# The routing stage of a mixture-of-experts step: VectorE's and TensorE's order around the last tiles, and where the Sigmoid table is loaded

## The reference

```python
mix = concatenate([rms_norm(attn, w_a), rms_norm(ssm, w_s)])
x = x + mix @ w_out                                  # called x1 here
h = rms_norm(x, norm_ffn_w)
score = sigmoid(h @ w_router)                        # 64 experts
idx = top_k(score + router_bias, 8)
g = 2.5 * score[idx] / sum(score[idx])
x = x + sum_e g_e * (silu(h @ w_gate[e]) * (h @ w_up[e])) @ w_down[e] + shared_expert(h)
```

## Time and profile before

| | |
|---|---|
| median of 3 runs | 1548.09 us (1543.95 to 1552.09) |
| profiled execution | 1553.29 us, span of the trace 1551.5 us |
| busy | PE 1376.6 us (89%), PEld 728.9 (47%), DVE 613.1 (40%), ACT 347.4 (22%), POOL 246.5 (16%) |
| chain that ended last | DMA 25% of the span, PE 20%; of it w_down transfers 24% |
| HBM | read 395.25 MB, written 41.06 MB, 281 GB/s over the span |

### The profile page before, as it was taken

How to read it: one execution, slowest core, us unless ns; L and a number is a source line. 1 busy time by engine, 2 the same in 40 slices (tenths; PEclk the granted TensorE clock), 3 DMA queues, 4 the chain that set the end, 5 groups by cost and what they waited for, 6 DMA issues and landing times. The chain is left out here.

```text
span 1551.5 us, 30198 instructions
## 1 busy us (share of the span) xinstructions
PE 1376.6 (89%) x9894; PEld 728.9 (47%) x9895; DVE 613.1 (40%) x1813; ACT 347.4 (22%) x939; POOL 246.5 (16%) x291
## 2 busy tenths in 40 slices
PE   6999799999999998699879787779999999999982
PEld 3445566666767775344633222223444443333320
DVE  1424255776486663333733222222333333332223
ACT  1202144444434444300101111111111111111110
POOL 1000200005363310000000111111222222211120
PEclk9999899999999999899879988889999999999996
DMA  8312399999989999650086999999875899999966
GB/s 305 66 27 57 104 310 302 349 338 325 318 294 315 336 333 338 231 197 28 7 344 223 371 370 372 372 369 370 326 220 177 297 319 313 380 370 357 370 233 201
DMA packets 160665, 424.08 MB, mean 273 GB/s; under 512 B 48209, under 2 KB 51826, under 8 KB 134386
## 3 DMA queue, kind: packets, MB, share of 16 engines
q1 hardware_dynamic: 142912, 381.30, 67.6%
q0 software_dynamic: 14400, 38.82, 10.4%
q10 hardware_dynamic: 3250, 2.65, 0.5%
HBM read 395.25 MB, written 41.06 MB: 281 GB/s over the span
## 5 line engine op out<-in xcount | busy, mean ns | idle before, releaser
L2555 PE MATMUL ps_gu<-ring,mixT 128*32 128x512 f32 (+2 forms) x1664 | 366.9, 636 | 57.1 <-SPq L2313 56.3
L2555 PEld LDWEIGHTS ps_gu<-ring,mixT 128*32 128x32 f32 (+2 forms) x1664 | 125.8, 141 | 293.6 <-issue 252.8
L2574 PE MATMUL ps_y<-w_dn,aT_e 128*32 128x512 f32 (+2 forms) x832 | 175.9, 598 | 4.5 <-DVE aT_e L2469 2.0
L1496 PE MATMUL ps_kT<-ident,ring 128*128 128x128 f32 x1024 | 142.3, 282 | 9.2 <-DVE ring L1129 4.9
L1496 PEld LDWEIGHTS ps_kT<-ident,ring 128*128 128x128 f32 x1024 | 115.3, 145 | 67.7 <-ACT ring L960 33.9
L2339 POOL DMA_INDIRECT kT<-h_dram,idx x50 | 51.9, 1038 | 583.0 <-DVE idx L2428 583.0
L2467 DVE TENSOR_TENSOR act_in<-sil,ps_gu 128x256 f32<-128x256 f32 x48 | 20.2, 421 | 295.0 <-ACT sil L2387 295.0
L1129 DVE COPY ring<-ps_kT 128x512 f32<-128x512 f32 x128 | 88.2, 689 | 88.1 <-PE ps_kT L1496 85.5
L2387 ACT ACTIVATE sil<-ps_gu 128x256 f32<-128x256 f32 x48 | 18.4, 384 | 401.0 <-PE ps_gu L2555 401.0
L2343 POOL DMA_INDIRECT sums_dram<-qT,sidx x48 | 76.5, 1593 | 147.8 <-DVE qT L2477 143.9
L2574 PEld LDWEIGHTS ps_y<-w_dn,aT_e 128*32 128x32 f32 (+2 forms) x832 | 55.4, 132 | 93.4 <-issue 85.7
(11 more groups left out here) (519 smaller groups left out, 1663.7 us busy)
## 6 DMA issues: line engine op xcount, KB each, us to landing
ring<-in_cache_k SPq DMA_DIRECT2D x256, 256.0 KB, 4.3
ring<-in_cache_v SPq DMA_DIRECT2D x256, 256.0 KB, 4.8
ring<-in_w_gate_e SPq DMA_DIRECT2D x64, 1024.0 KB, 8.8
ring<-in_w_up_e SPq DMA_DIRECT2D x64, 1024.0 KB, 11.8
w_dn<-in_w_down_e SPq DMA_DIRECT2D x64, 1024.0 KB, 9.8
w_in<-in_w_in SPq DMA_DIRECT2D x8, 1028.0 KB, 18.9
sums_dram<-w_dn SPq DMA_DIRECT2D x1, 4608.0 KB, 20.5
ring<-in_w_out SPq DMA_DIRECT2D x1, 4096.0 KB, 15.5
```

Of the source, the lines that this page charges most:

```text
L1496: last = pe.transpose(ps_kT[:, j % 2, e * PAGE:(e + 1) * PAGE], k_places[n % RING][:, e * DA + j * P:e * DA + (j + 1) * P], m.ident[:, :])
L2555: last = pe.matmul(ps_gu[at, :].rearrange("p (g n) -> p g n", g=2), xgT[:, u, k, at], w_gu[:, place, :, k, :].rearrange("p s g n -> p (s g ...
L2574: last = pe.matmul(ps_y[at, n, :], aT[:, j, at], w_dn[:, place, j, n * 512:(n + 1) * 512].rearrange("p s n -> p (s n)"), start=(j == 0), s ...
```

## The change

VectorE now handles x1 of tile t first and the hT copy of tile t-1 right behind it, ahead of the norm of tile t; the copy of the last tile stands after the loop. TensorE does router(3) before the last transposes instead of after. ScalarE gets one activation of one column with Sigmoid ahead of its wait for the router products; its result is written over a value that is no longer read.

```diff
--- before.py
+++ after.py
@@ -1918,6 +1918,7 @@
                         act.wait_ge(h_done, t)
                         if t >= 1:
                             act.wait_ge(h_out[(t + 1) % 2], 16 * ((t + 1) // 2))
+                act.activation(inv[:, 1, 0:1], m.ones[:, 0:1], ACT.Sigmoid)
                 act.wait_ge(iota_done, 1)
                 act.wait_ge(r_mm, TT)
                 act.activation(score[:, 0:PT, :].rearrange("p t e -> p (t e)"), ps[:, 7, 0:PT * NE], ACT.Sigmoid)
@@ -1948,6 +1949,16 @@
                 dve.reciprocal(inv[0:T_S, 2, 2 * PT:], inv[0:T_S, 1, 2 * PT:])
                 dve.wait_ge(misc_in, 32)
                 dve.wait_ge(x_again, 16 * TT)
+
+                def to_hT(t):
+
+                    n = rows(t)
+                    for half in range(2):
+                        dve.wait_ge(tr_mm, 2 * t + half + 1)
+                        c = m.col["norm_ffn"] + 4 * half
+                        w = m.columns[:, c:c + 4].unsqueeze(2).to_broadcast((P, 4, n))
+                        tt(hT[:, 4 * half:4 * half + 4, cols(t)], ps[:, half, :].rearrange("p (k n) -> p k n", n=P)[:, :, 0:n], w, ALU.mult).then_inc(hT_done, 1)
+
                 for t in range(TT):
                     n = rows(t)
                     for half in range(2):
@@ -1958,6 +1969,8 @@
                             at = slice(half * T_S, (half + 1) * T_S) if t == PT else slice(0, P)
                             last = dve.scalar_tensor_tensor(x1, ps[at, 2 + 2 * half + i, :], inv[0:n, 2, 2 * t + i:2 * t + i + 1], x1, ALU.mult, ALU.add)
                         last.then_inc(x1_done, 1)
+                    if t >= 1:
+                        to_hT(t - 1)
                     dve.wait_ge(ss_done, t + 1)
                     dve.tensor_scalar(st[0:n, 1, t:t + 1], st[0:n, 0, t:t + 1], 1.0 / D, EPS, ALU.mult, ALU.add).then_inc(ms2, 1)
                     dve.wait_ge(root2, t + 1)
@@ -1968,11 +1981,7 @@
                     dve.tensor_scalar(xn[0:n, t % 2, :], m.xres[0:n, t, :], st[0:n, 0, t:t + 1], None, ALU.mult).then_inc(xn2, 1)
                     dve.drain()
                     tt(h_row[0:n, t % 2, :], xn[0:n, t % 2, :], ffn_row[0:n, :], ALU.mult).then_inc(h_done, 1)
-                    for half in range(2):
-                        dve.wait_ge(tr_mm, 2 * t + half + 1)
-                        c = m.col["norm_ffn"] + 4 * half
-                        w = m.columns[:, c:c + 4].unsqueeze(2).to_broadcast((P, 4, n))
-                        tt(hT[:, 4 * half:4 * half + 4, cols(t)], ps[:, half, :].rearrange("p (k n) -> p k n", n=P)[:, :, 0:n], w, ALU.mult).then_inc(hT_done, 1)
+                to_hT(TT - 1)
 
                 over_experts = lambda x: x.unsqueeze(2).to_broadcast((P, TT, NE))
                 dve.wait_ge(iota_done, 1)
@@ -2228,8 +2237,8 @@
                         pe.wait_ge(misc_in, 32)
                     if t >= 2:
                         router(t - 2)
+                router(TT - 2)
                 transposes(TT - 1)
-                router(TT - 2)
                 router(TT - 1)
                 pe.wait_ge(m.ws_in, 32)
                 shared(0, 0, range(0, KD // 2), 0)
```

## The result

| | before | after |
|---|---|---|
| median of 5 runs | 1547.70 us (1543.95 to 1552.09) | 1532.67 us (1530.60 to 1540.98) |
| profiled execution | 1553.29, span 1551.5 | 1540.98, span 1539.3 |

The ratio is 0.9924, with a 95% interval from 0.9897 to 0.9950: between 7.7 and 15.9 us less, 11.8 in the middle.

The account below looks back on a forecast made before the run. The prediction took the routing chain, up to the start of the expert weight loads, to bound the kernel. Scores 14.4 us earlier, less 1.5 for the clock, gave 12.9 off the median 1548.09: 1535.2 us, range 1529.6 to 1543.9.

Parts of the forecast that it names:

- Part one: VectorE's x1 ahead of the hT copy: TensorE's three projection waits go, the last tile's x1 starts 12.8 us earlier.
- The half clock: TensorE at 1.2 GHz behind two waits for x1: 3.0 us and, in the sample tile, 1.7 counted as saved.
- rival 1: The clock gives less: no half clock in the median run, or new idles cost their full bound; 1539.9 us, chance 0.20.
- Part two: TensorE's router(3) ahead of the last transposes: costs VectorE nothing, gains nothing while VectorE is last; bounds 0 and 0.9 lost.
- part three: Sigmoid table loaded early on ScalarE: VectorE's copies are last, so worth 0 by itself; bounds 0 and 1.28 us.
- With slow routers the copies move too: Last routers at half clock: transposes and hT(4) also come 0.9 us later, so VectorE's index copies stay last.
- The ranks and the clock: TensorE idles of 2.0 and 2.3 us before routers and ranks may lower the clock; 1.5 us taken off, bounds 0 and 6.1.
- The second idle: TensorE between the shared product's end at 739.2 and the ranks at 741.5: idle 2.3 us, where it idled 0.74.
- The bound for the idle before the ranks: If the clock falls there: 2.2 us in the 40 rank instructions, up to 3.0 in the shared matmuls behind.
- The end hangs on when the expert weights begin to flow: SP's first expert load, after its wait for the routing tables, sets the run's end; it would move 12.9 us, to 767.4.
- Rival 2: Gain absorbed: the expert stage starts no earlier, its transfers paced by something that doesn't move; 1548 us, chance 0.06.
- Rival 3: TensorE's clock falls before router(3), staying at 1.2 GHz through ranks and shared products: 20.7 us lost, 1554.4, chance 0.04.

Follow-up runs that it names:

- before_b: The kernel before, unchanged, executed once more to see the clock in another execution; 1544.18 us (one run), 69.1 us from start of transposes(0) to first rank matmul.
- x1_only: The changed kernel with the Sigmoid activation and router(3)'s move taken back, only x1 ahead of the copy; 1534.99 us, ratio 0.9927 to the kernel before.
- x1_table: The changed kernel with only router(3) put back behind the last transposes, the early Sigmoid activation kept; 1545.42 us (one run).
- after_filler: The changed kernel with two extra unread matmuls in TensorE's idle of 1.95 us ahead of router(3); 1537.86 us, ratio 0.9944 to the kernel before.
- loads_6_late: The changed kernel with SP waiting for the middle of the last shared products before the first expert weights; 1532.37 us, ratio 0.9897 to the kernel before.
- loads_late: The changed kernel with SP waiting for the end of the shared products before the first expert weights; 1540.63 us, ratio 0.9965 to the kernel before.
- before_c: The kernel before, unchanged, in a third execution; 1542.50 us (one run), 69.2 us from start of transposes(0) to first rank matmul.

## Why the prediction was right, and where not

The forecast was 12.9 us less, 1535.2; the medians show 15.0 less, 1532.67, the ratio 11.8. Size and sign were right, but the size by errors that cancel. Against before_b the stage gives 69.1 - 56.9 = 12.2 us, and the forecast of 12.9 comes to it like this: 2.6 too much for half clock that only the profiled execution had; 0.6 too little up to the scores, which came 68.7 - 53.7 = 15.0 us earlier and not 14.4; 1.3 too little behind them, where 0.2 was lost and 1.5 had been taken off. That these make up for one another is luck. By its steps:

**Part one.** The layout held. The last tile's x1 was to start 725.7 - 684.27 = 41.4 us from the origin and started 727.14 - 686.25 = 40.9. All three waits went, and hT(3) hid behind the square at no cost: from x1(4) to the variance step it is 742.98 - 738.46 = 4.52 us before and 731.67 - 727.14 = 4.53 after. The waits on the first half's signal held up nothing.

**The half clock, 4.7 us of the sum,** was mis-sized as a property of the kernel. For the 1.7 of the sample tile its cause, the wait, fits every trace: with the wait it took 8.52 to 8.78 us in four executions of four, without it, or with filler in it, 7.09 in nine of nine. But the 3.0 behind the wait of 2.70 occurs in one execution of four. The text took it from one trace into the median; it named this under rival 1 as a doubt and argued against it with "three of three". The 12.2 of a typical execution are near the ratio's 11.8. The 15.0 between the medians lies inside the interval, and no run explains its excess.

**Part two and part three at 0** was wrong. Together they are worth 58.8 - 56.9 = 1.9 us at the ranks. "With slow routers the copies move too" holds only if router(3) stands ahead of the transposes. With it behind, hT(4) and the copies keep their time, the routers alone are late, and the scores come 1.79 us after the copies. The text also left out TensorE's own queue: with both routers behind the transposes, the shared product starts later, at half clock, and ends after the mask (by 0.5 us in x1_only, 1.6 in x1_table). So the table edit alone moved the ranks by 0.1, and the place of router(3) by 1.8. The routers of 5.57 behind the transposes could be read from the earlier trace rows. In this change, with all three parts, the copies were last as forecast, so the sum didn't suffer. That the table edit adds nothing once router(3) is moved, no run tests; the trace after speaks for it: the scores are there at 738.15, with a load of 1.28 ahead it would be 739.43, and the copies keep VectorE until 739.95 (an estimate). The load of 1.28 with its activation 0.01 behind it (732.07, 733.36), and the scores 1.2 earlier by hiding it, agree with the trace of before. The load itself starts 0.02 us behind the activation ahead of it (731.85, 0.20 us long), so there is no gap on that side either. No run here shows the drain of some 1.38 us that the Trainium skill has ("ScalarE: Activation LUTs", section "What ACT_TABLE_LOAD costs").

**The ranks and the clock.** Forecast were idles of 2.0 and 2.3 us; the first was 1.95, and the clock fell behind it, in this kernel and in all three others that had it (routers of 2.30 to 2.41 us), and not in the two where filler took its place (2.00). It was to cost 0.9 us; by the distance of after_filler it cost 0.5, in the last hT copy, which starts and runs later. The second idle never came to be: the slow shared product filled it, and TensorE waited 0.69. So of the 1.5 us taken off some 0.5 was lost. The bound for the idle before the ranks was sound: after_filler, where it exists, lost 3.5 in the ranks and 1.3 behind them, 4.8 against 5.2 in the text. The price per rank instruction of 0.055 us was too low, though: the last 30 of the 40 took 7.10 us at half clock (739.27 to 746.37) and 3.86 at full clock in before (757.16 to 761.02), which is 0.11 more for each.

**What bounds the kernel.** "The end hangs on when the expert weights begin to flow" fell. The first loads have at least 5 us of room (loads_6_late), and holding up the engines' start into the expert stage by 8.8 us, with the loads 16.4 us late, cost some 6 (loads_late). Both fit TensorE's chain through the shared products as what sets the end; no run delays that chain alone. The sum wasn't touched, because both hang on the ranks. How much of the gain is left at the end can't be read from single traces: from the origin to the end it is 867.2 us in before, 856.6 in before_b, 860.4 in before_c and 853.1 after. The ratio has to say it.

**The rivals.** Rival 1 was half of the truth: the longer slow stretch was in fact rare, and errors the other way made up for it. Rival 2's case, loads that don't matter, is real in the first loads and harmless. Rival 3's fall of the clock around router(3) happened; it lasted some 7 us and not into the ranks.

## What to carry to other kernels

If an engine waits for a copy that waits for another engine, put first whatever frees the buffer the next big piece of work needs. When two edits lie on one chain, look at every queue that meets at its end: here the scores moved by 1.2 us and the ranks by 0.1. A stretch of half clock in one trace is an event of that execution until a second trace shows it too: count it apart from the waits in the sum. And before filling or shortening an idle of TensorE, look at the next one: here the fall of the clock was moved from thin work (0.5 us on the path) to the ranks (4.3 us).

## What the runs showed of the hardware

Behind the same wait of 2.70 us ahead of a projection the clock was at 1.2 GHz in one execution of four. Behind 2.54 to 2.55 us it was in four of four, and behind 1.95, ahead of small matmuls, in four of four. Behind 0.88 it never was (five of five). The length of the idle alone therefore doesn't decide. Nor does the fall need an idle: behind twenty one-column instructions, with TensorE busy all the time, it came in three executions of thirteen, and in x1_table once more directly behind the ranks (the shared product there took 5.40 us instead of 3.70). Where extra matmuls of 1.7 or 2.6 us filled a wait, the work behind it ran at 2.4 GHz in each of the four places; one of the four, the wait of 2.70, doesn't count for much. Rank matmuls of 64 columns take 0.13 us each at 2.4 GHz (3.86 / 30) and 0.24 at 1.2 GHz (7.10 / 30, after_filler), a little less than twice as long.
